# A one-core transformer block with 16 experts: the first expert job is gathered on its own and written out before the loop, the sorting pass stands inside it, and a modulation product moves to an earlier stage

## The reference

```
mod   = silu(c) @ w_mod + b_mod                 # six rows of 2048: shift, scale, gate, twice
z     = modulate(rmsnorm(x), mod[0], mod[1]) @ w_in       # attention, gMLP and convolution columns
out   = concat(attention(z), gmlp(z), conv(z)) @ w_out
h     = x + mod[2] * out
m     = modulate(rmsnorm(h), mod[3], mod[4])
idx   = top-2 of 16 experts inside the best group of 4 (sigmoid scores, bias for the choice)
y     = sum over the two chosen e of gate_e * ((silu(m @ w_gate[e]) * (m @ w_up[e])) @ w_down[e])
result = h + mod[5] * y                         # mod[5] is the "FFN gate" below
```

## Time and profile before

| | |
|---|---|
| median of three runs | 1549.53 us |
| profiled execution, its own time | 1542.42 us |
| profiled execution, span from first to last instruction | 1540.6 us |
| TensorE busy, mean granted clock | 84%, 0.915 of full speed |
| VectorE, ScalarE, POOL busy | 28%, 10%, 5% |
| bytes moved | 559.75 MB, 363 GB/s on average |

### The profile page before, as it was taken

How to read it: one execution, slowest core, us unless ns; L and a number is a source line. 1 busy time by engine, 2 the same in 40 slices (tenths; PEclk the granted TensorE clock), 3 DMA queues, 4 the chain that set the end, 5 groups by cost and what they waited for, 6 DMA issues and landing times.

```text
span 1540.6 us, 19541 instructions
## 1 busy us (share of the span) xinstructions
PE 1288.9 (84%) x7844; PEld 528.6 (34%) x7845; DVE 432.2 (28%) x797; ACT 158.1 (10%) x253; POOL 80.2 (5%) x143
## 2 busy tenths in 40 slices
PE   3899998999999898789789889978677875975976
PEld 2556544554444433223233233232131221321321
DVE  3122697766563411111010110121111101111112
ACT  3000102232000140000000000000000000000000
POOL 0112001112231000000000000000000000000000
PEclk9999999999999998789899989999888977986997
DMA  9999424676897869999899999999999999999996
GB/s 381 419 412 405 183 82 160 224 273 237 325 352 290 332 249 391 422 421 421 341 422 420 421 399 421 421 396 421 418 420 420 422 421 418 421 421 419 421 421 265
DMA packets 84373, 559.75 MB, mean 363 GB/s; under 512 B 9728, under 2 KB 9728, under 8 KB 22592
## 3 DMA queue, kind: packets, MB, share of 16 engines
q1 hardware_dynamic: 69408, 502.49, 79.7%
q0 software_dynamic: 14304, 51.76, 9.1%
q10 hardware_dynamic: 576, 4.19, 0.7%
HBM read 556.31 MB, written 2.10 MB: 362 GB/s over the span
## 4 chain that ended last, share of the span: by engine, by line
PE 52%; DMA 35%; issue 6%; DVE 5%; ACT 2%; SPq 1%; DVEq 0%; ACTq 0%; POOL 0%
PE ps L820 12%; DMA ring<-w_gate_dram 9%; DMA ring<-w_up_dram 9%; DMA rope_heads<-w_down_dram 8%; PE ps L815 7%; PE ps L571 7%; PE ps L842 5%; PE ps L674 3%; DMA ring<-w_half_dram 3%; DMA ring<-w_in_dram 3%; PE ps L565 2%; PE ps L836 2%; PE ps L791 2%; PE ps L760 2%; PE ps L576 2%
## 5 line engine op out<-in xcount | busy, mean ns | idle before, releaser
L815 PE MATMUL ps<-ring,early 128*32 128x256 f32 x2304 | 179.3, 456 | 88.4 <-issue 35.7
L820 PE MATMUL ps<-ring,early 128*64 128x512 f32 x672 | 163.5, 625 | 38.8 <-issue 33.0
L1429 DVE TENSOR_TENSOR big<-ps,big 128x1024 f32<-128x1024 f32 x68 | 80.1, 1219 | 372.1 <-PE ps L791 372.1
L571 PE MATMUL ps<-ring,big 128*128 128x512 f32 x320 | 146.5, 600 | 0.0
L815 PEld LDWEIGHTS ps<-ring,early 128*32 128x32 f32 x2304 | 74.7, 126 | 206.9 <-issue 97.5
L1096 DVE SCALAR_TENSOR_TENSOR halves<-ring,silu_c,halves 128x1024 f32<-128x1024 f32 x96 | 123.1, 1283 | 41.3 <-DMA ring<-w_half_dram 35.4
L674 PE MATMUL ps<-ring,big 128*128 128x512 f32 x256 | 115.3, 607 | 1.3 <-ACT big L995 1.3
L820 PEld LDWEIGHTS ps<-ring,early 128*64 128x64 f32 x672 | 45.7, 143 | 142.1 <-issue 124.2
L571 PEld LDWEIGHTS ps<-ring,big 128*128 128x128 f32 x320 | 59.5, 192 | 68.5 <-issue 68.4
L674 PEld LDWEIGHTS ps<-ring,big 128*128 128x128 f32 x256 | 49.3, 196 | 64.3 <-issue 64.3
L791 PE MATMUL ps<-halves,early 64*128 64x512 f32 x272 | 67.8, 617 | 0.0
(11 more groups left out here) (314 smaller groups left out, 1054.6 us busy)
## 6 DMA issues: line engine op xcount, KB each, us to landing
ring<-w_gate_dram SPq DMA_DIRECT2D x128, 1024.0 KB, 24.0
ring<-w_up_dram SPq DMA_DIRECT2D x64, 1024.0 KB, 22.6
ring<-w_down_dram SPq DMA_DIRECT2D x64, 1024.0 KB, 23.9
ring<-w_half_dram POOLq DMA_DIRECT2D x96, 512.0 KB, 6.6
ring<-w_mix_dram SPq DMA_DIRECT2D x32, 1024.0 KB, 11.4
big<-w_up_dram SPq DMA_DIRECT2D x32, 1024.0 KB, 27.1
big<-w_down_dram SPq DMA_DIRECT2D x32, 1024.0 KB, 20.4
ring<-w_in_dram SPq DMA_DIRECT2D x28, 1024.0 KB, 8.7
```

The lines of the kernel that those rows point to most:

```text
L571: mm = pe.matmul(ps[:, b + t, :], nT[:, k, t * P:(t + 1) * P], w, start=(k == 0), stop=(k == KT - 1))
L815: mm = pe.matmul(out_b[0][BASE * f:BASE * (f + 1), :], rows[0][:, k, :], w[:, kk, f * 256:(f + 1) * 256], start=(k == 0), stop=(k == KT - 1))
L820: mm = pe.matmul(out_b[1][REST * f:REST * (f + 1), :], rows[1][:, k, :], w[:, kk, f * N:(f + 1) * N], start=(k == 0), stop=(k == KT - 1))
L1429: tt(y, banks[:, 2 * h:2 * h + 2, :].rearrange("p a n -> p (a n)"), y, ALU.add).then_inc(done, 1)
```

## The change

1. The 16 gate steps stand in the stages of K and V: three behind each chunk of `KV_`, two behind each of the first two chunks of `Q1_`. They write bank `M`. The bias comes over POOL's queue, already laid out over partitions (`b_gate`, 256 KiB), and VectorE adds it with one operation on 512 columns. The bias product, two of POOL's half-row preparations and three fills with zeros are gone.
2. After the logits TensorE does both steps "gate_b", then 16 steps "first": they multiply the tokens with a one-hot matrix of 96 columns (`oh_first`) for expert 15 alone, round three banks; ScalarE writes them straight to `xg`. The steps "route" 2 to 4 stand behind the 5th, 9th and 13th.
3. VectorE makes `oh_first` as soon as the places are known, and `oh_all` only when the table is ready.
4. Every engine's body of the first job is written out ahead of the loop (again in three versions), and the loop starts at job 1. The first job has no scatter. Between its gate products and its up products stands `sort_rows`, the 16 gathers of 512 columns with their copies on ScalarE.

```diff
+            if g == KV_:
+                seq += [("gate", 3 * c + i) for i in range(3)]
+            elif g == Q1_ and c < 2:
+                seq += [("gate", 12 + 2 * c + i) for i in range(2)]
...
-    seq += [("hT", 3)] + gate[8:9] + [("logits", 3)] + gate[9:13] + [("route", 1)] + gate[13:16]
+    seq += [("hT", 3), ("logits", 3), ("gate_b", 0), ("gate_b", 1), ("route", 1)]
     for k in range(KT):
-        seq.append(("gather", k))
-        if k in (0, 2, 5):
-            seq.append(("route", 2 + (0, 2, 5).index(k)))
-        seq += [("gate_b", (k - 8) // 2)] * (k in (8, 10))
+        seq.append(("first", k))
+        if k in (4, 8, 12):
+            seq.append(("route", 1 + k // 4))
...
+            pool.wait_ge(ext_done, 8)
+            pool.dma_start(modrow[:, 1, :], b_gate[:, :]).then_inc(gate_bias_in, 16)
...
-                        pe.wait_ge(modcol_saved, 8)
+                        pe.wait_ge(gate_saved, 1)
...
+                elif kind == "first":
                     k = step[1]
                     if k == 0:
+                        pe.wait_ge(first_ready, 1)
+                        pe.wait_ge(bcast_saved, 6)
+                    elif k > 2:
+                        pe.wait_ge(first_saved, k - 2)
+                    bank = (S[0], S[1], M)[k % 3]
                     for t in range(TT):
+                        mm = pe.matmul(bank[:, 0:BLK], tokens[:, t, k * P:(k + 1) * P], oh_first[:, t, :],
                                        start=(t == 0), stop=(t == TT - 1))
...
+            def sort_rows():
+                pe.wait_ge(oh_ready, 1)
+                for k in range(KT):
+                    if k > 1:
+                        pe.wait_ge(sorted_saved, k - 1)
+                    for t in range(TT):
+                        mm = pe.matmul(S[k % 2], tokens[:, t, k * P:(k + 1) * P], oh_all[:, t, :],
+                                       start=(t == 0), stop=(t == TT - 1))
+                    mm.then_inc(sort_done, 1)
...
                 for m, out_b in ((0, Gb), (1, Ub)):
-                    if m == 1:
+                    if m == 1 and first:
+                        sort_rows()
+                    elif m == 1:
                         scatter(j, 0)
...
-            with pe.Fori(0, jobs) as j:
+            any_job(0, True)
+            with pe.Fori(1, jobs) as j:
+                any_job(j, False)
...
+            dve.wait_ge(gate_bias_in, 16)
+            dve.wait_ge(slot_free, used_chunk(NUMBER["gate", KT - 1]))
+            tt(modrow[:, 1, :], M, modrow[:, 1, :], ALU.add).then_inc(gate_saved, 1)
             for h in range(NH):
...
+            first = rt[:, 15, :, FIRST_EXPERT]
+            tt(small[:, 10:12], first, rs_tok[:, 0:2], ALU.mult).then_inc(dve_step, 1)
...
+            for t in range(TT):
+                last = ts(oh_first[:, t, :], k_("slots")[:, 0:BLK], rt[:, 19, t, FIRST_EXPERT:FIRST_EXPERT + 1],
+                          small[:, 10 + t:11 + t], ALU.is_equal, ALU.mult)
+            last.then_inc(first_ready, 1)
```

More of the change, by code:

```diff
@@ L86, in make_schedule @@
     seq += [("spatial",), ("bcast", 0), ("bcast", 1)]
[L88 to L91, removed]
+    after = {(0, 0): [("bcast", 2), ("bcast", 3)], (0, 1): [("gated",)], (0, 3): [("half", 2)], (1, 3): [("half", 3)],
+             (2, 2): [("half", 4)], (3, 0): [("half", 5)], (3, 1): [("shift",), ("logits", 0)],
+             (3, 2): [("logits", 1)], (3, 3): [("shift_rows",), ("logits", 2)]}
     for g in range(4):
@@ L171, with build @@
 CONST_COLS = CONST_AT["cos"][0]
[L174 removed]
+def build(nc, x, ctx, params, consts, b_half, b_gate, w_mix, w_half, w_gmod, w_in, w_out, w_gate, w_up, w_down, out):
     with ExitStack() as stack:
@@ L822, in experts @@
                         mm.then_inc(slot_free, 1)
-                scatter(j, 1)
+                if not first:
+                    scatter(j, 1)
                 pe.wait_ge(hidden_ready, j + 1)
@@ L1028, in job_rows, with job_evac @@
                 return copy(xg, span[:, :, 0:BLK]).then_inc(xg_ready, 1)
-            def job_evac(j, parts, at):
+            def job_evac(j, parts, at, first):
+                for k in range(KT if first else 0):
+                    act.wait_ge(sort_done, k + 1)
+                    act.activation(xg_all[:, k, :], S[k % 2], ACT.Identity, bias=modcol[:, 3, k, 0:1],
+                                   scale=scale_ffn[:, k:k + 1]).then_inc(sorted_saved, 1)
                 act.wait_ge(slot_free, j * JCH + used_job(7))
@@ L1363, in _ @@
             link(nc.vector.tensor_reduce(place4, both, AX.X, ALU.add))
-            for t in range(TT):
-                ts(oh_all[:, t, :], k_("slots"), place4[:, 0, t:t + 1], rs_tok[:, t:t + 1], ALU.is_equal, ALU.mult)
-                last = ts(oh_more[:, t, :], k_("slots"), place4[:, 1, t:t + 1], rs_tok[:, t:t + 1],
-                          ALU.is_equal, ALU.mult)
-            link(last)
-            tt(oh_all, oh_all, oh_more, ALU.add).then_inc(oh_ready, 1)
             link(nc.vector.tensor_copy(vcol[:, 8:9], T[0:CAND, 128:129]))
@@ L1416, in _ @@
             dve.wait_ge(table_ready, 1)
+            for t in range(TT):
+                ts(oh_all[:, t, :], k_("slots"), place4[:, 0, t:t + 1], rs_tok[:, t:t + 1], ALU.is_equal, ALU.mult)
+                last = ts(oh_more[:, t, :], k_("slots"), place4[:, 1, t:t + 1], rs_tok[:, t:t + 1],
+                          ALU.is_equal, ALU.mult)
+            link(last)
+            tt(oh_all, oh_all, oh_more, ALU.add).then_inc(oh_ready, 1)
+            dve.wait_ge(oh_ready, 1)
             def spread_matrix(j, i, slots):
@@ L1439, in hidden_product @@
                 last.then_inc(hidden_ready, 1)
-                add_rows(j, 1, summed)
+                if first:
+                    dve.wait_ge(bcast_saved, 6)
+                else:
+                    add_rows(j, 1, summed)
                 dve.wait_ge(ehT_done, j + 1)
```

139 lines of the change are left out of this document (70 added, 69 removed).

## The result

The changed kernel takes 1566.05 us (median of four, 1565.72 to 1572.79), the kernel before 1550.47 beside it: a ratio of 1.0109, 95% interval 1.0078 to 1.0141. Forecast were 1546.8 us and 1539.5 to 1556, so the range is missed by 10 us on the slow side. The profiled executions lie further apart, 1542.42 and 1566.21 us, because that of before was a quick one.

The account below looks back on a forecast made before the run. TensorE's chain up to the first job, then the weight stream at about 421 GB/s, was taken to bound the kernel. Terms 14.8 - 6.9 - 26.8 + 16.2 = -2.7 us moved the median from 1549.5 to 1546.8 us, range 1539.5 to 1556.

Parts of the forecast that it names:

- Term a: Stages of K and V: the added gate's 128 instructions lengthen TensorE's unbroken work by 14.8 us, bounds 14.5 and 16.
- Term b: Output projection to logits: the gate's leaving gives back 6.9 us, bounds -5.6 and -9.5.
- Term c: From the places to the first job: 42.5 us shrink to 15.7, so -26.8 us, bounds -30 and -10.4.
- one dip of 1.7 us: In the gathers ahead of the first job: allowance for one fall of the clock after routing's idle time, 1.7 us.
- The 2.5 us for the route steps: Between places and first job: about 2.5 us of routing steps on TensorE were taken to stay.
- The bound of -10.4: Places to first job, slow case: gathers all at 1.2 GHz, +6.3 us, and the longest entry pause, +10.1 us.
- Term d: First job: 27.5 us of sorting free no slot, so the weight stream gets a 16.2 us hole, bounds 15 and 22.
- the last sentence of part d: Job loop: TensorE catches up within job 1, and from job 2 on all is as before, shifted; no added cost.
- the holes behind the jobs fall otherwise: Job loop: sign that the prediction is wrong; such holes counted among gains in the 0.35 chance shared with the clock staying up.
- The second: Entry into the first job: a 13.8 us pause replaces 3.7, giving 1557 us; chance 0.21, shared with slow gathers and more dips.
- The clock did not stay up: Rival, projection to first job: no clock falls, warm gathers, short entry, -8.5 us, 1541 us; chance 0.35, shared with similar gains.
- The sorting pass was not hidden: Rival, first job: the stream has enough chunks ahead to close the sorting hole, 1531 us; chance 0.02.

Follow-up runs that it names:

- the run of the first job alone: Kernel before plus the separately gathered, written-out first job with its sorting pass; gate chunks and bias in old places, 5 never-run products: 1556.06 us, ratio 1.0035.
- the run with 8 never-run products: Changed kernel with 8 products that are never executed added ahead of its loop, so the loop's code begins at instruction 7,037: 1551.05 us, ratio 0.9995.
- The runs with the place repaired: Changed kernel with its loop's code moved by 8 or 27 never-run products: ratios 0.9995 and 0.9992 to the kernel before.
- its two harmless copies: Kernel before with 1 and with 120 never-run products behind a branch ahead of the job loop: 1553.74 us (0.9991) and 1556.93 us (1.0022).
- 27 never-run products: Changed kernel with 27 products that are never executed ahead of its loop, which then begins at instruction 7,113: 1548.39 us, ratio 0.9992.
- with 110: Kernel before with 110 never-run products ahead of its loop, whose code begins 440 instructions further on; same executed work: 1577.73 us, ratio 1.0166.
- changed with two bodies: Changed kernel with the 33-to-64-row body taken out of TensorE's loop, those rows left out, no never-run products: 1552.69 us, ratio 0.9995.
- with 391: Changed kernel with 391 never-run products in the 96-row version of the first job, loop at instruction 8,569: 1584.99 us, ratio 1.0202.
- the run with the sorting pass spread out: Changed kernel with 8 never-run products and one sorting step behind each of the first job's 16 gate and up chunks: 1552.38 us, ratio 1.0001.
- the gate alone: Kernel before with only the gate moved to the K and V stages and its bias added on VectorE; gathers, sorting, loop unchanged: 1558.24 us, ratio 1.0046.
- the three runs with two bodies: 33-to-64-row body left out of TensorE's loop: kernel before 1542.55 us (0.9925), changed kernel 1552.69 (0.9995), changed kernel with 17 never-run products 1539.09 (0.9940).

## Why the prediction was wrong

*Term a, +14.8.* Measured 15.2 (247.21 to 262.41), of which 14.5 are left at the projection's first product (371.92 and 386.42), and the wait behind it 6.86 in place of 6.85 us, as predicted. Transfers had room: 265 GB/s.

*Term b, -6.9.* From the projection's first product to the end of the last logits (525.4 and 531.5) it took 153.5 us before and 145.1 after: -8.4, within the bounds. Both terms together were tested alone: +7.1 against 7.9.

*Term c, -26.8.* Measured: the same stretch, 42.5 us before, is 540.39 to 561.84, 21.5 us: -21.1. Two summands were too small. Gathers and route steps took 14.6 us where 11.2 were counted, because over half of the gathers ran at 1.2 GHz and I had added one dip of 1.7 us. (The 2.5 us for the route steps don't follow from their own summands, 33.7 - 27.5 - 3.0, which leave 3.2; they took 2.9.) What was overlooked is that the gate's move itself seems to have done this. With the gate in its old place (the run of the first job alone) its last products stand between the idle time of the routing and the gathers, and those ran at full clock:

```profile
545.40:557.00 11.60, 11.60 (x102) 9.27 (x98) 4.63 (x19) 7.00 (x16) 0.00 (x0) 1.00 1.01 421
```

In the changed kernel only small products of the routing stand between, and the granted clock was 0.50 in the gathers from 541.2 to 550.0; in the run with 8 never-run products it was the same. The entry took 6.0 us in place of 3.7. The bound of -10.4 was not needed.

*Term d, +16.2.* The ninth slot came free 599.99 - 561.84 = 38.2 us into the job (38.1 predicted), eight issues lay before it, and 586 to 600 shows 3 GB/s. The hole is the forecast one.

*The sum.* +14.5 - 8.4 - 21.1 + 16.2 = +1.2 us, and job 2 starts 1.8 us later. Against the -2.7 of the prediction the mis-sized term is c, by 5.7 us; b gave back 1.5 of it. With only that the median would have been about 1551 us, inside the range. The runs with the place repaired say the same: 0.9995 and 0.9992. The first job's start scatters from one execution to the next by more than this (576.8 to 589.9 us in the profiled executions of before and its two harmless copies), so such sums, from one execution each, hold to a few us; that the four parts cancel rests on the runs with the place repaired.

*The step that failed* is the last sentence of part d: "so from job 2 on the picture is that of before, shifted." I took the pauses at the entries as a property of the jobs. They are a property of where the code stands, and the change moved it by 2,530 instructions: 21.9 us of pauses ahead of jobs 3, 5 and 7 became 45.4, and the stream lost 39.7 us there in place of 11.9. Shown by undoing it (1551.05 and 1548.39 us with 8 and 27 never-run products) and by making it in the kernel before (1577.73 with 110).

The prediction did name "the holes behind the jobs fall otherwise" among the signs of being wrong, but it counted that only as a possible gain, and put no price on longer pauses in the loop.

*The rivals.* The second had the right mechanism, a longer pause at a branch, in the wrong place: it was priced once, at the first entry, which came out at 6.0 us (+2.3), far from 13.8. What decided stood in the same rows, entries of the loop, one of which I had already shown to open a hole in the stream. The clock did not stay up. The sorting pass was not hidden.

*Open* is the rule from place to number of packets. Counted from a multiple of 256, loops at 56 and 57 (before with 110; changed with two bodies) had the long pauses, and so had 93 and 121 (the changed kernel; with 391); those at 96, 108, 123 to 127, 132 and 201 the short ones. 121 against 108 contradicts a simple threshold. Nor does the place alone decide the later entries: the run with the sorting pass spread out has its loop where the run with 8 never-run products has it, with the same pauses ahead of jobs 3, 5 and 7 within 1.1 us, but from job 8 on its pauses are 6.3 to 6.5 us where the other has up to 13.7. The two kernels' code ahead of the loop differs, and my count may be off by a constant between them. No trace shows which packets are fetched; that they are TensorE's is inferred, since only its code was moved. Why the first job alone and the gate alone don't add up is argued from one trace, not shown.

## What to carry to other kernels

When a change adds, removes or duplicates code ahead of a long loop with several bodies, list the pauses at the loop's entries and the packets on the instruction queue in them, before and after, and build the changed kernel at a second place with some never-run instructions before judging it: here this alone moved one kernel from 1548 to 1585 us. Don't add the pauses up, though. Such a pause costs where all slots are full, since then nothing refills the stream (45.4 us of pauses, 39.7 us lost), and next to nothing where slots are free (12.69 us at 420 GB/s). And when a piece of work is spread over a stream to close a hole, look for what waits behind its last piece: the hole can come back there.

## What the runs showed of the hardware

- A pause at an entry grows with the packets fetched: in the kernels with three bodies and at jobs 3, 5 and 7 one took 4.5 to 5.7 us, three 9.4 to 11.7, five 14.6 to 16.3 (up to 18.0 in the run with 391): about 5.5 us and 2.5 more for each further packet. At later entries one took up to 6.9 and three up to 13.8 (17.5 in the run with 391). Traffic is not needed for it: in the changed kernel the second half of the window over the pause before job 3 passed at 0 to 39 GB/s, and the first entry of the kernel before, 3.73 us with one packet, had nothing else moving.
- Ten never-run products fewer, 40 instructions, made the kernel before 1.4% slower (1.0022 to 1.0166).
- In the three runs with two bodies, where the same body follows itself from job 8 on, two have a pause at job 8 (6.7 and 7.2 us, one packet), and behind it there is a single one, of 8.0 us. At jobs 3, 5 and 7, behind a job with another body, there were packets with 2,379 instructions in the loop always, and with 1,887 at some. Alternating bodies don't always bring them: the changed kernel alternates 64 and 32 rows from job 8 on and shows one packet in the last 514 us.
- Over the loop (640 to 1540 us) the slower kernel fetched 34 packets and the faster one 53.
